# Moving part of an attention output projection into the page steps of a decoder kernel on one core

## The reference

```
# prompt, per head h (8 heads of 2 x 64 features, values of 128):
s = q . k - slope[h] * (qpos - kpos), masked above the diagonal      # for both halves
a = softmax(s_first) - lam * softmax(s_second);  o = a @ v
# sample: the same over 2048 cached positions (16 pages of 128 rows per sequence, read through
# page_table) plus the 4 new ones, merged page by page
o = rmsnorm(o, b_subln_w, 1e-5) * (1 - lam_init)        # per head
h = h + o.reshape(B, T, 1024) @ b_w_o                   # output projection, 1024 x 1024
x = rmsnorm(h, norm_ffn_w)                              # then router logits, top 2 of 16 experts
h = h + moe(x)
```

## Time and profile before

| what | value |
|---|---|
| median of 2 runs | 1433.45 us (1431.74 to 1435.17) |
| the profiled execution, time | 1434.65 us |
| its span in the trace | 1432.9 us |
| TensorE busy, share of the span | 1274.6 us, 89% |
| VectorE / ScalarE / GpSimd busy | 700.4 / 421.7 / 173.1 us |
| TensorE's granted clock, mean | 0.938 of full |
| data moved | 348.27 MB, mean 243 GB/s |

### The profile page before, as it was taken

The page is one execution under the profiler, slowest core; times in us unless marked ns, Lnnn a source line. Parts: engine busy times, 40 slices in busy tenths (PEclk is TensorE's granted clock), DMA queues, the critical chain, the costliest instruction groups (busy, mean ns, idle before and its releaser), DMA issues. The chain is left out here.

```text
span 1432.9 us, 31639 instructions
## 1 busy us (share of the span) xinstructions
PE 1274.6 (89%) x12696; PEld 743.6 (52%) x12696; DVE 700.4 (49%) x1883; ACT 421.7 (29%) x1136; POOL 173.1 (12%) x251
## 2 busy tenths in 40 slices
PE   8999999996998998939999999677787799999887
PEld 4445555544557555535555455455554355755453
DVE  5345757685654121257244353588755565321123
ACT  3034556553111211143112202244446211121112
POOL 2012332331010000021022000110000001000002
PEclk9999999998997999969999999998879899799998
DMA  6152453347318999963467899899989613899925
GB/s 240 59 154 61 128 174 84 84 146 238 149 46 320 374 364 355 356 249 105 149 242 298 298 362 388 319 407 408 386 328 351 252 60 122 319 378 359 349 73 188
DMA packets 133909, 348.27 MB, mean 243 GB/s; under 512 B 22603, under 2 KB 52478, under 8 KB 125566
## 3 DMA queue, kind: packets, MB, share of 16 engines
q1 hardware_dynamic: 115378, 311.53, 60.4%
q10 hardware_dynamic: 13388, 16.82, 3.5%
q0 software_dynamic: 4992, 17.83, 3.3%
HBM read 302.61 MB, written 43.52 MB: 242 GB/s over the span
## 5 line engine op out<-in xcount | busy, mean ns | idle before, releaser
L449 PE MATMUL bank<-wring,xT 128*128 128x512 f32 x448 | 200.9, 602 | 1.9 <-DVE xT L430 1.1
L449 PEld LDWEIGHTS bank<-wring,xT 128*128 128x128 f32 x448 | 84.1, 192 | 101.4 <-issue 100.1
L1523 PE MATMUL bank<-wring,xT 128*128 128x512 f32 x256 | 118.9, 618 | 2.0 <-DVE xT L1443 2.0
L949 PE MATMUL bank<-xT,wring 128*128 128x512 f32 x256 | 113.6, 601 | 4.0 <-DVE hgrn_g L766 4.0
L2892 DVE STREAM_TRANSPOSE attn_k_pages<-attn_k_pages 128x1024 f32<-128x1024 f32 x64 | 77.6, 1232 | 43.5 <-DMA attn_k_pages<-cache_k 43.1
L949 PEld LDWEIGHTS bank<-xT,wring 128*128 128x128 f32 x256 | 48.7, 193 | 65.3 <-issue 59.6
L1523 PEld LDWEIGHTS bank<-wring,xT 128*128 128x128 f32 x256 | 49.2, 198 | 59.2 <-issue 59.1
L2892 DVE STREAM_TRANSPOSE wring<-wring 128x1024 f32<-128x1024 f32 x44 | 52.8, 1224 | 45.2 <-DMA wring<-cache_k 45.2
L2401 PE MATMUL bank<-xT,wring 128*128 128x512 f32 x128 | 58.1, 607 | 0.0
L1745 DVE TENSOR_TENSOR attn_qo<-attn_qo,bank 128x128 f32<-128x128 f32 x32 | 7.8, 283 | 83.5 <-ACT attn_qo L1696 83.5
L1745 DVE TENSOR_TENSOR hgrn_g<-hgrn_g,bank 128x128 f32<-128x128 f32 x32 | 7.7, 284 | 79.3 <-ACT hgrn_g L1696 79.3
(11 more groups left out here) (478 smaller groups left out, 2377.0 us busy)
## 6 DMA issues: line engine op xcount, KB each, us to landing
attn_k_pages<-cache_k SPq DMA_DIRECT2D x64, 512.0 KB, 7.6
wring<-cache_v SPq DMA_DIRECT2D x56, 512.0 KB, 7.8
wring<-cache_k SPq DMA_DIRECT2D x44, 512.0 KB, 7.0
moe_wd<-moe_w_down SPq DMA_DIRECT2D x20, 1024.0 KB, 12.9
attn_shared<-cache_v SPq DMA_DIRECT2D x40, 512.0 KB, 5.7
wring<-moe_w_gate SPq DMA_DIRECT2D x18, 1024.0 KB, 11.7
wring<-moe_w_up SPq DMA_DIRECT2D x18, 1024.0 KB, 13.6
wring<-a_w_in SPq DMA_DIRECT2D x16, 1024.0 KB, 9.2
```

The costliest lines, as they stand in the source:

```text
L449: last = nc.tensor.matmul(bank[:, :], xT[:, c, cols(t)], w[:, c, :], start=(c == 0), stop=(c == DC - 1))
L949: last = nc.tensor.matmul(bank[:, :], lhsT, k.xT[:, c, 0:SEQ], start=(c == 0), stop=(c == DC - 1))
L1523: last = nc.tensor.matmul(bank[:, :], k.xT[:, c, cols(t)], w[:, c, :], start=(c == 0), stop=(c == DC - 1))
```

## The change

Four things change together, all in layer 1.

1. **Projections earlier.** `PROJECT_AT` gives slots 0 to 9 two units each and slots 10 to 13 one. The prompt attention starts in slot FIRST = 14, so its 20 units end in slot 33. V_EARLY and K_IN_VALUES become 7.
2. **Units by tile.** First the eight units of tiles 0 and 2, then four of tile 1, then eight of tile 3. The biases are made anew for each group (24 instead of 8, on GpSimd).
3. **Late work in the page steps.** When a tile's heads are complete, VectorE and ScalarE form its rmsnorm factors (`late_mean_out`, `late_root`, `late_inverse`), ScalarE scales in place (`late_scale`), TensorE turns in two halves through the bank that p_turn uses (`late_turn`), and ScalarE copies back with the gain (`late_turned_out`, at the end of its slot, behind the next unit's `p_exps`). This happens in slots 23, 24, 27 and 35 for tiles 0, 2, 1, 3. In slots 24, 25 and 28 TensorE projects columns 0 to 511 of tiles 0, 2, 1 (`late_project`), and VectorE adds in the slot after (`late_add`). The weights for it (2.1 MB) are one more transfer and keep value buffer 5 until then, so that two value buffers are left: `values_in(v)` waits for value(v - 2). The placed sample output is added up in SBUF (`add_placed`), since its bank is used for the late work.
4. **A new tail.** `MixOutTail` replaces `MixOut` in layer 1. Prompt tiles need no scaling, turning or copying; TAIL_PARTS has seven products instead of ten: (0,1), (2,1), (1,1), (PT,1), (PT,0), (3,1), (3,0).

```diff
-PROJECT_AT = {0: (4, 5), 1: (6, 7), 2: (8, 9), 3: (10, 11), 4: (12,), 5: (13,), 6: (14, 15), 7: (16,), 8: (17, 18), 9: (19,),
-              **{s: (s + 10,) for s in range(10, 18)}}
-K_IN_VALUES = 9
-V_EARLY = 11
-VALUE_SLOT = [2] * (V_EARLY - 2) + [0, 2] + [(0, 1, 5)[(s - V_EARLY) % 3] for s in range(V_EARLY, STEPS - 4)] + [3, 4, 5, 1]
-UNITS = [unit for h in range(0, HEADS, 2) for unit in
-         (((h, 3),), ((h, 0), (h, 2)), ((h, 1), (h + 1, 1)), ((h + 1, 3),), ((h + 1, 0), (h + 1, 2)))]
-FIRST = 18
+PROJECT_AT = {**{s: (2 * s + 4, 2 * s + 5) for s in range(10)}, **{s: (s + 14,) for s in range(10, 14)}}
+K_IN_VALUES = 7
+V_EARLY = 7
+VALUE_SLOT = [2] * (V_EARLY - 2) + [0, 2] + [(s - V_EARLY) % 2 for s in range(V_EARLY, STEPS - 4)] + [3, 4, 1, 5]
+UNITS = [((h, 0), (h, 2)) for h in range(HEADS)] + [((h, 1), (h + 1, 1)) for h in range(0, HEADS, 2)] + [((h, 3),) for h in range(HEADS)]
+FIRST = 14
+LATE = (0, 2, 1, 3)
+LATE_SCALE = {FIRST + HEADS + 1: 0, FIRST + HEADS + 2: 1, FIRST + HEADS + HEADS // 2 + 1: 2, FIRST + 2 * HEADS + HEADS // 2 + 1: 3}
+LATE_PROJECT = {24: (0, 0), 25: (1, 0), 28: (2, 0)}
...
+                def late_project(s, x, n):
+                    pe.wait_ge(late_w_in, 32 * (n + 1))
+                    pe.wait_ge(late_act, late_out(2 * (x + 1)))
+                    if late_projects(s):
+                        pe.wait_ge(late_added, late_projects(s))
...
+                    for c in range(DC):
+                        last = nc.tensor.matmul(LATE_BANK[:, :], late_o(LATE[x])[:, c, :], late_w[:, c, :], start=(c == 0), stop=(c == DC - 1))
+                    last.then_inc(late_projected, 1)
...
+                    if s in LATE_TURN:
+                        late_turn(s, LATE_TURN[s], 0)
+                    if s in LATE_PROJECT:
+                        late_project(s, *LATE_PROJECT[s])
+                    if s in LATE_TURN:
+                        late_turn(s, LATE_TURN[s], 1)
...
                     if v_s == V_EARLY + 1:
+                        late_weights(0)
+                        sp.wait_ge(valued, V_EARLY + 1)
                         values_in(V_EARLY + 2)
                     v_s = s - LAG
                     if v_s >= V_EARLY + 3:
-                        sp.wait_ge(valued, v_s - 2)
+                        sp.wait_ge(valued, v_s - 1)
                         values_in(v_s)
...
+TAIL_ORDER = (0, 2, 1, PT, 3)
+TAIL_PARTS = ((0, 1), (2, 1), (1, 1), (PT, 1), (PT, 0), (3, 1), (3, 0))
...
+        sample_means()      # MixOutTail.vector
+        sample_scale()
+        add(0)
+        turned_out()
+        norm(0)
+        routing.tables(dve, ch)
+        add(1)
+        norm_out(0)
+        pick(0)
+        norm(1)
+        add(2)
+        norm_out(1)
+        slots(0)
+        pick(1)
+        add(3)
+        add(4)
+        norm(2)
+        norm_out(2)
+        slots(1)
+        pick(2)
+        norm(3)
+        add(5)
+        norm_out(3)
+        slots(2)
+        pick(3)
+        add(6)
+        norm(4)
+        slots(3)
+        norm_out(4)
+        pick(4)
+        slots(4)
```

More of the change, by code:

```diff
@@ L1359, in gpsimd @@
         self.k.order_n["gpsimd"] = ch.n
-        for i, t in enumerate(ORDER):
+        for i, t in enumerate(self.order):
             pool.wait_ge(routing.slots_ready, i + 1)
@@ L2057, in _ @@
             ffn.experts.tensor(pe)
[L2058 removed]
+            pe.wait_ge(ffn.mix.added, ffn.mix.parts)
             for t in range(2):
@@ L2222, in values_landed @@
     def values_landed(self, s):
-        slot = VALUE_SLOT[s]
-        return self.v_in[slot], 16 * GROUP * VALUE_SLOT[:s + 1].count(slot)
+        sem = self.v_sem[VALUE_SLOT[s]]
+        return self.v_in[sem], 16 * GROUP * [self.v_sem[slot] for slot in VALUE_SLOT[:s + 1]].count(sem)
     def page(self, sp, s, r):
@@ L2619, in parts_of, with bias_at, last_with_bias, late_turns @@
         at = at + (i + 1) * P
-def last_of(h):
-    return max(n for n, unit in enumerate(UNITS) if h in [head for head, i in unit])
+def bias_at(n, h):
+    return (0 if n < HEADS else HEADS if n < HEADS + HEADS // 2 else 2 * HEADS) + h
+def last_with_bias(m):
+    return max(n for n, unit in enumerate(UNITS) if m in [bias_at(n, h) for h, i in unit])
+LATE = (0, 2, 1, 3)
+LATE_GROUPS = ((0, 2), (1,), (3,))
+LATE_UNITS = (HEADS, HEADS + HEADS // 2, 2 * HEADS + HEADS // 2)
+LATE_MEANS = {FIRST + n: i for i, n in enumerate(LATE_UNITS)}
+LATE_SCALE = {FIRST + HEADS + 1: 0, FIRST + HEADS + 2: 1, FIRST + HEADS + HEADS // 2 + 1: 2, FIRST + 2 * HEADS + HEADS // 2 + 1: 3}
+LATE_TURN = dict(LATE_SCALE)
+LATE_PROJECT = {24: (0, 0), 25: (1, 0), 28: (2, 0)}
+def late_turns(s):
+    return 2 * sum(at < s for at in LATE_TURN)
+def late_act_before(s):
+    return sum(at < s for at in LATE_SCALE) + sum(at < s for at in LATE_MEANS) + late_turns(s)
+def late_scaled(x):
+    s = [at for at, y in LATE_SCALE.items() if y == x][0]
+    return late_act_before(s) + 1
+def late_rooted(i):
+    s = [at for at, y in LATE_MEANS.items() if y == i][0]
+    return late_act_before(s) + (s in LATE_SCALE) + 1
+def late_out(n):
+    s = list(LATE_TURN)[(n - 1) // 2]
+    return late_act_before(s) + (s in LATE_SCALE) + (s in LATE_MEANS) + (n - 1) % 2 + 1
+def late_projects(s):
+    return sum(at < s for at in LATE_PROJECT)
 def units_at(s):
@@ L2838, in _ @@
                     ends = v_s >= GROUPS_ and v_s % GROUPS_ == 0
-                    if ends:
-                        place(v_s // GROUPS_ - 1)
                     for n in units_at(s):
@@ L2852, in _ @@
                             p_values(n)
+                    if ends:
+                        place(v_s // GROUPS_ - 1)
+                    if s == FIRST:
+                        turn_gain()
+                    if s in LATE_TURN:
[4 more added lines that the diff above has]
+                        late_turn(s, LATE_TURN[s], 1)
                 place(DEC_B - 1)
@@ new lines, in take_gain, with late_add @@
+                def take_gain():
+                    dve.wait_ge(late_turned, 1)
+                    nc.vector.tensor_copy(gain, LATE_BANK[:, 0:1]).then_inc(late_ready, 1)
+                def late_add(x, n):
+                    dve.wait_ge(late_projected, late_projects([s for s, p in LATE_PROJECT.items() if p == (x, n)][0]) + 1)
+                    part = k.h[:, LATE[x], n * HB:(n + 1) * HB]
+                    nc.vector.tensor_tensor(part, part, LATE_BANK[:, :], ALU.add).then_inc(late_added, 1)
@@ L3068, in new_out, with late_root, late_scale, late_turned_out @@
                     nc.scalar.activation(AT[0:DEC_T, PAGES, :], TURNED[0:DEC_T, 0:QUAD], ACT.Copy).then_inc(new_at_out, 1)
+                def late_root(i):
+                    act.wait_ge(late_ready, MEAN_READY[i])
+                    nc.scalar.activation(late_means[i][:, 1, :, :], late_means[i][:, 0, :, :], ACT.Sqrt).then_inc(late_act, 1)
+                def late_scale(x):
+                    t = LATE[x]
+                    act.wait_ge(late_ready, RSTD_READY[[t in group for group in LATE_GROUPS].index(True)])
+                    for h in range(HEADS):
+                        part = late_o(t)[:, h, :]
+                        last = nc.scalar.activation(part, part, ACT.Copy, scale=late_rstd[t][:, h:h + 1])
+                    last.then_inc(late_act, 1)
+                def late_turned_out(s, x, n):
+                    act.wait_ge(late_turned, 1 + late_turns(s) + n + 1)
+                    act.wait_ge(late_ready, GAIN_READY)
+                    part = slice(n * (DC // 2), (n + 1) * (DC // 2))
+                    nc.scalar.activation(late_o(LATE[x])[:, part, :], P_TURNED[:, :].rearrange("p (c n) -> p c n", n=P), ACT.Copy, scale=gain)\
+                        .then_inc(late_act, 1)
                 ffn.scalar(act)
```

351 lines of the change are left out of this document (309 added, 42 removed).

## The result

The changed kernel took 1471.47 us (median of 2 runs, 1467.52 to 1475.43) against 1433.45: a ratio of 1.0265 with a 95% interval of 1.0135 to 1.0395. The prediction said 1442.4 and no change to be seen, with a range up to 1462. Rival C (late projections starve the transfers) named 1467.

The account below looks back on a forecast made before the run. TensorE was taken to bound the early page slots and transfers, nearly, the late ones. 1434.65 profiled plus 1.8 (page steps) plus 7.1 (output projection) gave 1443.6; the median lies 1.2 lower, 1442.4 us, range 1417 to 1462.

Parts of the forecast that it names:

- Rival C: Page steps: late projections in slots 23 to 28 starve the transfers; stage +23.8, tail +10.1, 1467 us; chance 0.14.
- Late work: Page steps, slots 23 to 28: late projections and turns mostly hidden beside VectorE's work; 5 us taken, slot 31 at 1080.
- slot 14: Page steps: early slots bound by TensorE, so this slot, the first with attention, starts at 888.6 us.
- the first attention slot: Page steps: values(8) and keys(15) wait for the last projection as before, 18.4 us, next slot at 907.0.
- the end: Page steps from slot 31: 22.8 us with units, then 14 us without; last place at 1116.8, 1.8 us later.
- Slots 15 to 30: 10.5 each: Page steps: 16 slots between 10.1 and 10.9 us, 168 us before late work.
- the lower bound: Page steps: transfers alone, 42 groups including the late weights, put the last place at 1105.7, or -9.3.
- bounds of 0 and 23: Late work: 0 if queued transfers absorb it; 23 if all 13.5 us and both waits in slots 23 and 27 count.
- The tail: Output projection: one chain between TensorE and VectorE, 117.4 us with clock losses, 7.1 more than before.
- five named waits: Output projection: TensorE waits in the new chain of about 4, 7, 9.5, 7 and 9 us.
- upper bound of 120.4 us: Output projection: 103.4 us at full clock plus 1.8 + 3.8 x 4 for slow clock.
- Rival B: Output projection: removed work is all gain, tail ends at 78.0 us, -32.3; total 1403 us; chance 0.05.

Follow-up runs that it names:

- e5: Kernel before with only the projections and first attention slot moved earlier, three value buffers, no late work; 1.0050 of the kernel before.
- e12: Changed kernel with seven of eight matmuls of each late product left out and their weights not loaded; 1.0179 of the kernel before.
- e1: Changed kernel with seven of eight matmuls of each late product left out, weights still loaded; 1.0160 of the kernel before.
- e2: Changed kernel with ScalarE's copy of the first turned half ahead of the next unit's exponentials; 1.0239 of the kernel before.
- e7: e6 plus the order changes of e2 (copy ahead of exponentials) and e3 (norm ahead of pick); 1.0079 of the kernel before.
- e4: Kernel before with two value buffers instead of three in the late page steps; 1.0031 of the kernel before.
- e6: Changed kernel with late products in slots 32 to 34, weights loaded once after value(24), three value buffers until group 24; 1.0247 of the kernel before.
- e3: Changed kernel with norm(i + 1) ahead of pick(i) on VectorE in the tail; 1.0143 of the kernel before.
- e9: e3 plus, on TensorE in the tail, the next projections ahead of place and gather; 1.0109 of the kernel before.
- e13: Changed kernel with late products in pieces avoiding slots 26 and 30, edits of e2 and e9, VectorE's tail adds ahead of picks; 0.9916 of the kernel before.

## Why the prediction was wrong

**The failed step is the one headed "Late work", the sentence "I take 5".** The steps ended at 1142.1 instead of 1116.8, 25.3 us late. Term by term: slot 14 began at 892.1 instead of 888.6 (+3.5, of which 2.3 were there at slot 4); the first attention slot took 18.7 instead of 18.4; slots 15 to 30 took 192.2 instead of 173 (+19.2); the end 39.2 instead of 22.8 + 14 (+2.4).

**"Slots 15 to 30: 10.5 each" was right.** e5, without late work, has 168.4 us for them (with three value buffers; e12, with two, has 10.7 us a slot in slots 15 to 22). So the late work was 23.8 us in this execution, 24 to 27 over four. The stretches give its parts: the weights' transfer 5 to 8 (e12), the three products in slots 24, 25 and 28 11 to 14 (100.5 less 83.8, the waits and the rest; and e1), the two half-turn waits 4 to 5 (e2, e7), the rest 1.7 (e7 against e5).

**Two errors made the 5.** The first is an omission. The weights' transfer (2.1 MB) stood in the lower bound and in no term, though the earlier trace rows had just said that in these slots a transfer is time. The second is the choice between bounds of 0 and 23. I argued that VectorE can go on while TensorE projects, so that the products are hidden. They are not: in slots 24, 25 and 28 TensorE is never idle, and they last 16.2, 15.7 and 15.0 us, what the prediction's own sum gave them (15, 16 and 14). The slots behind do not win it back. SyncE issues a page group only when its buffer's product is done, and that product stands in TensorE's list behind the lump, so the transfers fall to 300 and 169 GB/s. The upper bound of 23 agrees with the measured 23.8 by luck. Its 13.5 us for the three slots was right (11 to 14), but the two waits in it, the other 9.5 us, were 4 to 5, and the weights' 5 to 8 us were not in it.

**Rival C was right in its number, half right in its mechanism.** Page scores late, SyncE waiting 50 us where e5 has 22, DMA at 337 GB/s: yes. "With two value buffers": where no product stands in the way the number of buffers changed nothing, by e4, and by slots 15 to 23 of e12 (two buffers, 85.7 us) and e6 (three, 84.7); whether a third would have helped behind the lumps is not shown. What makes the slots long is the lump of 7 us in a slot that has 2 to 3 to spare. Its +23.8 for the steps is the upper bound above, and meets the measured +23.4 by the same luck.

**The tail was right in its mechanism, 2 us short in its size.** Predicted +7.1, measured +9.1 from the last place to the experts' first product. Four of the five named waits came as written, the fifth smaller. The lists side by side were enough to see it, and e3, e9 and e13 show the cause by taking it away in three steps: 123.6, 106.9, 101.1, 85.4. The Trainium skill's rule (TensorE: Matmul & The Clock Gate, section HAM oscillation: a loop in which TensorE waits in between drops to half rate and pays at every restart) stood for the upper bound of 120.4 us, +10.1. The trace agrees, though here TensorE waits for VectorE where the page's loop waits for transfers: +9.1 is nearer to that than to my +7.1, at a mean clock of 0.74, and with most of the waits filled (e13) the mean was 0.86.

**Rival B's tail is nearly reached by another order.** "The removed work is all gain" asked for 32.3 us less; e13 has 28.8 less than before, with the same products and turns as the changed kernel.

**What stays open:** the 7 us of e5's ratio, which its trace does not show; whether the slots behind the lumps would have won more back with the transfers full, or with a third value buffer; and why one transfer costs more than its 5.3 us (8.1 in slots 15 to 23, 5.9 in slot 23 of e13 against e7).

## What to carry to other kernels

When a stretch is bound by transfers that wait on an in-order engine's products, price each lump of work on that engine by what exceeds the time left in its own slot, and price each added transfer in full; where work has to be moved into such a stretch, it goes in pieces that fit the slots. Here three lumps of 7 us cost 11 to 14 us and the same matmuls in pieces about 4 to 5, and the weights' transfer stayed a cost in both. When work is taken out of a stage, first ask what it was covering: write the lists of the two engines side by side, and put the step that the other engine needs next (norm) ahead of the one that it needs later (pick). Here the order alone was worth 38 us (123.3 to 85.4), more than the 25.1 us of work removed.

## What was not expected of the hardware

A lower clock adds to an order's price. In the tail 25 us of TensorE work were removed, and 12 came back as slower execution: two of the routing gathers took 3.71 us each in the changed kernel and 2.00 in e13. And executions of the same page steps differ by 8 us, some 5 of it ahead of slot 15 (242.2 to 247.0 us from the first page scores), while each later stretch repeats within 2.5 us.
